# Taking the norm of 256 memory rows inside the last fox pair of a streaming encoder step, and turning the memory columns one projection earlier

## The chip, the cores and the metric

One core of a Trainium2 chip runs the whole program. The metric is the device time of one execution in microseconds (us). Three executions of the kernel before are shown, and one more was recorded by the hardware profiler.

## What is computed

The program is one inference step of a one-layer encoder on 1056 frames (a prompt of 1024 and a sample of 32), with 1024 model columns. What matters here is the part that reads the 256 memory rows:

```python
def _mem_kv(mem, g_mem, w_mem_kv, gk_mem):
    bsz, n, _ = mem.shape
    kv = _rmsnorm(mem, g_mem) @ w_mem_kv
    mk, mv = jnp.split(kv, [MEM_DIM], axis=-1)
    mk = _head_rms(mk.reshape(bsz, n, MEM_HEADS, HEAD_DIM), gk_mem)
    return mk, mv.reshape(bsz, n, MEM_HEADS, HEAD_DIM)
```

`_rmsnorm` divides each memory row by the root of its mean square and multiplies by a gain per column. The layer around it is: a SwiGLU feed-forward block, a norm, one combined projection (a gated convolution of 256 channels, "fox" attention of 8 heads with a forget gate, memory cross-attention of 4 heads), the output projection, a second SwiGLU block and a last norm. Every product is kept near fp32 precision by splitting both factors into a high and a low part and adding three products (hi x hi, hi x lo, lo x hi).

## The kernel before

The kernel is written with one instruction stream per engine, and the order on each engine is the order of the code. TensorE (PE) has the first feed-forward block, two conv groups, four fox pairs of two heads each (`attend(g)`, g = 0 to 3, NG = 4), two memory pairs (`mem_pairs`), the output projection and the second feed-forward block. Engines meet in counting semaphores: `wait_ge(sem, n)` holds an engine's whole stream until the count is there.

**A fox pair** has nine projections, then rows of scores whose maxima VectorE (DVE) takes (`smax(0)` to `smax(17)`), and then 28 blocks n = 0 to 27. For each block PE forms the keyed scores (`keyed(n)`, lines L2782 to L2785), ScalarE (ACT) the exponentials (`exps(n)`, L1480), and PE weighs the values with them (`weigh(n)`, L2814), two blocks behind: the loop runs keyed(n), weigh(n - 2). The outputs gather in PSUM banks. DVE then divides six parts (`mixed(0)` to `mixed(5)`: a reciprocal of the sums at L2254 and a product at L2258), as their last blocks are weighed: after blocks 6, 11, 20, 21, 22 and 27. Each part adds 2 to the count `A["mixed"]`. Block 17 is the sample's first one of the second head, 32 columns wide, and its output goes to bank 0, which part 0 frees; so PE waits for both counts of part 0 there:

```python
                    if q0 == SEQ and first:
                        pe.wait_ge(A["cv_loaded"], 32 * g + 32)
                        if j:
                            pe.wait_ge(A["mixed"], 12 * g + 2)
```

**The memory rows** lie in two tiles by token, `memtok[0]` (a piece of `raw`, shown as w_raw) and `memtok[1]` (mem_by_token), loaded long before. Before the change their norm is the start of the memory pairs. ACT squares and sums both tiles (`memory_rough`, L1538), DVE makes the mean (L2283), ACT the rough root of it (`rough`: a logarithm at L1121 and an exponential at L1123), DVE refines it in three tiny steps (`rstd`, L1736 to L1740) and scales both tiles (L2287). PE turns them by 16 transposes (`turn_memory`, L2651) behind the second of the memory pair's projections, (0,1). They go to banks 3, 4, 5 and 7, of which 4 and 5 hold outputs of the last fox pair until its part 5 is divided (`A["mixed"]` at 12 * NG). DVE multiplies the turned columns by the gain (`memory_gain`, L2180) into the two halves of `memf`: columns 0 to 3 over `mixf` (shown as mix_f), columns 4 to 7 over `vT`. `mixf` has to be stored first (`MIX["stored"]`, an SP transfer at L799). ACT rounds each half (`memory_hi`, L1545), and GpSimd (POOL) takes what is left (L1072, shown as memT_lo).

**What waits for them on PE**: projection (0,2) waits for both halves of the gain (`mp["dve"]` at 6), and the key projection (0,3), which multiplies the memory, for both low halves (`mp["lo"]` at 2). Halfway through each projection PE sums the head squares of the one before (`mem_sums`, L2874).

**POOL** splits weights: a CAST for the high part and a TENSOR_TENSOR for the low one. In the last fox pair it does `split_in` for the first memory pair and then `split_second(0, 1)` and `split_second(1, 2)` (L1060, L1062), four instructions that start when the weights of the second memory pair have landed.

## Time and profile before

| | before |
|---|---|
| three executions, us | 2075.45, 2075.93, 2077.22 |
| median, us | 2075.93 |
| the profiled execution's own time, us | 2075.1 |
| its span in the profile, us | 2073.3 |
| mean granted TensorE clock | 0.994 |
| PE busy | 2019.5 us, 97% of the span |
| DVE busy | 1342.2 us, 65% |
| ACT busy | 967.8 us, 47% |
| POOL busy | 452.5 us, 22% |

All positions below are microseconds from the start of the span. The last fox pair's 28 blocks take 1130 to 1166, the memory pairs 1166 to about 1258. A row of the timeline has its start, its length, the engine, the line, the operation, the tile written and the tiles read, their sizes, how many instructions are merged, and in brackets how long the engine was idle before it and what ended that. PE matmuls overlap each other in these rows. PEclk is the granted share of TensorE's full clock.

### The profile page before, as it was taken

The numbers are of one execution on the slowest core, as the hardware profiler recorded it, in microseconds if no ns is written. First come the engines' busy times: TensorE is split into PE (matmuls) and PEld (weight loads), VectorE is DVE, ScalarE is ACT, GpSimd is POOL, SyncE is SP. The second block draws the span as 40 slices with busy tenths as digits, with TensorE's granted clock in tenths as the row PEclk, the third lists the DMA queues.
The fourth block names the chain that finished last, engine by engine and source line by source line (L and its number), as shares of the span: only waits on it lengthen the run. The fifth ranks groups of instructions, "written<-read, shape, count | busy, mean of one in ns | idle before, by whom it ended". The sixth has DMA issues, their size and how long they took to land.

```text
span 2073.3 us, 35667 instructions
## 1 busy us (share of the span) xinstructions
PE 2019.5 (97%) x14062; PEld 1929.0 (93%) x14062; DVE 1342.2 (65%) x2065; ACT 967.8 (47%) x1643; POOL 452.5 (22%) x225
## 2 busy tenths in 40 slices
PE   5999999999999999999999999999999999999998
PEld 5999999999999999877868779999999999999997
DVE  7999647994415673656666785699965599623323
ACT  6556434654334431445445572266544466533423
POOL 0000000003665744011011342000000000266662
PEclk8999999999999999999999999999999999999999
DMA  7554324555746344621111244064523265474732
GB/s 228 132 148 134 102 64 132 161 155 183 238 162 224 133 156 42 100 78 37 52 48 52 62 159 141 9 203 138 154 85 93 83 189 144 156 259 167 247 133 114
DMA packets 296852, 274.51 MB, mean 132 GB/s; under 512 B 29864, under 2 KB 238888, under 8 KB 296432
## 3 DMA queue, kind: packets, MB, share of 16 engines
q1 hardware_dynamic: 296688, 272.25, 43.7%
q8 instruction: 113, 1.85, 0.4%
q14 instruction: 51, 0.42, 0.1%
HBM read 222.41 MB, written 49.80 MB: 131 GB/s over the span
## 4 chain that ended last, share of the span: by engine, by line
PE 87%; DVE 6%; ACT 3%; issue 1%; another core or an unknown queue 0%; DVEq 0%; ACTq 0%
PE banks L277 26%; PE banks L278 26%; PE banks L279 26%; PE banks L2814 3%; DVE scores_minusF L2245 1%; PE banks L2782 1%; PE banks L2783 1%; PE banks L2736 1%; ACT k_hi_twice L1436 1%; ACT head_r L1121 0%; DVE head_rstd L1738 0%; DVE head_rstd L1736 0%; DVE head_rstd L1740 0%; DVE kT L2210 0%
## 5 line engine op out<-in xcount | busy, mean ns | idle before, releaser
L277 PE MATMUL banks<-hforms_hi,w_hi 128*128 128x264 f32 x2112 | 601.4, 285 | 10.8 <-DVE hforms_lo L1940 6.8
L278 PE MATMUL banks<-hforms_lo,w_hi 128*128 128x264 f32 x2112 | 601.6, 285 | 0.0
L279 PE MATMUL banks<-hforms_hi,w_lo 128*128 128x264 f32 x2112 | 600.3, 284 | 0.0
L1001 POOL TENSOR_TENSOR w_lo<-w_raw,w_hi 128x1024 fp32r<-128x1024 f32 x132 | 321.5, 2439 | 1196.6 <-ACT w_hi L1231 1196.6
L277 PEld LDWEIGHTS banks<-hforms_hi,w_hi 128*128 128x128 f32 x2112 | 398.1, 188 | 14.5 <-issue 7.9
L279 PEld LDWEIGHTS banks<-hforms_hi,w_lo 128*128 128x128 f32 x2112 | 397.4, 188 | 0.0
L278 PEld LDWEIGHTS banks<-hforms_lo,w_hi 128*128 128x128 f32 x2112 | 397.1, 188 | 0.1
L277 PE MATMUL banks<-acts_a,w_hi 128*128 128x352 f32 x960 | 309.9, 323 | 0.0
L279 PE MATMUL banks<-acts_a,w_lo 128*128 128x352 f32 x960 | 309.2, 322 | 0.0
L278 PE MATMUL banks<-acts_a,w_hi 128*128 128x352 f32 x960 | 309.0, 322 | 0.0
L1231 ACT ACTIVATE w_hi<-w_raw 128x1024 fp32r<-128x1024 f32 x132 | 139.5, 1058 | 282.9 <-PE banks L279 259.9
L277 PE MATMUL banks<-h_hi,w_hi 128*128 128x352 f32 x576 | 198.7, 345 | 5.2 <-DVE vT L2180 3.0
L279 PE MATMUL banks<-h_hi,w_lo 128*128 128x352 f32 x576 | 186.6, 324 | 0.0
L278 PE MATMUL banks<-h_lo,w_hi 128*128 128x352 f32 x576 | 186.3, 323 | 0.0
L277 PEld LDWEIGHTS banks<-acts_a,w_hi 128*128 128x128 f32 x960 | 180.3, 188 | 0.2
L278 PEld LDWEIGHTS banks<-acts_a,w_hi 128*128 128x128 f32 x960 | 180.3, 188 | 0.2
L279 PEld LDWEIGHTS banks<-acts_a,w_lo 128*128 128x128 f32 x960 | 180.2, 188 | 0.0
L1163 ACT ACTIVATE w_hi<-w_raw 128x512 fp32r<-128x512 f32 x228 | 142.6, 625 | 54.0 <-PE banks L279 51.8
L1163 ACT ACTIVATE w_hi<-w_sums 128x1024 fp32r<-128x1024 f32 x112 | 118.5, 1058 | 82.0 <-PE banks L279 75.5
L1834 DVE TENSOR_TENSOR w_lo<-w_raw,w_hi 128x512 fp32r<-128x512 f32 x228 | 155.8, 684 | 0.1
L1959 DVE TENSOR_TENSOR acts_a<-acts_f,acts_a 128x704 fp32r<-128x704 f32 x60 | 107.1, 1795 | 59.4 <-ACT acts_a L1219 59.4
L1843 DVE TENSOR_TENSOR w_lo<-w_sums,w_hi 128x1024 fp32r<-128x1024 f32 x112 | 136.4, 1218 | 1.2 <-ACT w_hi L1163 0.9
(343 smaller groups left out, 3560.1 us busy)
## 6 DMA issues: line engine op xcount, KB each, us to landing
w_raw<-in_w_ffn_down SPq DMA_DIRECT2D x132, 512.0 KB, 3.7
w_raw<-in_w_ffn_gate SPq DMA_DIRECT2D x76, 512.0 KB, 5.3
w_raw<-in_w_ffn_up SPq DMA_DIRECT2D x76, 512.0 KB, 5.1
act_rows<-act_f SPq DMA_DIRECT2D x44, 528.0 KB, 3.0
acts_f<-act_rows SPq DMA_DIRECT2D x66, 352.0 KB, 4.1
w_raw<-in_w_in SPq DMA_DIRECT2D x20, 512.0 KB, 5.7
x_spill<-xT SPq DMA_DIRECT2D x4, 2112.0 KB, 10.0
xT<-x_spill SPq DMA_DIRECT2D x6, 1408.0 KB, 9.1
```

The lines of the kernel that those rows point to most:

```text
L277: eng.matmul(out, w_hi, x_hi, start=first, stop=False, skip_group_check=added)
L278: eng.matmul(out, w_hi, x_lo, start=False, stop=False, skip_group_check=added)
L279: return eng.matmul(out, w_lo, x_hi, start=False, stop=last, skip_group_check=added)
L1001: pool.tensor_tensor(wlo[:, wd_slot(e), :], raw[:, wd_slot(e), :], whi[:, wd_slot(e), :].bitcast(F32), ALU.subtract)\
L1163: act.activation(slots(whi, wxh, G[q], n), src, ACT.Copy).then_inc(f[f"{which}_hi"], 1)
L1231: act.activation(whi[:, wd_slot(e), :], raw[:, wd_slot(e), :], ACT.Copy).then_inc(f["wd_hi"], 1)
L1436: act.activation(KS1[half_rows(j), j, s:s + w], kT[half_rows(j), s:s + w], ACT.Copy)\
L1834: dve.tensor_tensor(slots(wlo, wxl, slot, 1), r[:, at:at + 1, :], slots(whi, wxh, slot, 1).bitcast(F32), ALU.subtract).then_inc(f[f"{which ...
L1843: dve.tensor_tensor(slots(wlo, wxl, slot, 2), SS[:, 2 * part:2 * part + 2, :], slots(whi, wxh, slot, 2).bitcast(F32), ALU.subtract)\
L1959: dve.tensor_tensor(acts(p)[:, 1, :, :], astg[:, m % 4, :, :], acts(p)[:, 0, :, :].bitcast(F32), ALU.subtract).then_inc(f["act_lo"], 1)
L2245: dve.tensor_tensor_reduce(junk[0:rows, 0:w], PS[0:rows, b:b + w], nF[0:rows, j, k0:k0 + w], 1.0, -3e38, ALU.add, ALU.max, m).then_inc(A[" ...
L2814: pe.matmul(PS[:, 512 * ob + oc:512 * ob + oc + w], VO[0:kr, vo, j, :], PRT[0:kr, (b0 + n) % 4, 0:w], start=first, stop=last, skip_group_c ...
```

## The change

Four things are moved, and no instruction is added or taken away on any engine.

1. ACT's two squares of the memory rows go from the start of the memory pairs into the last fox pair, ahead of the third piece of maxima (`maxima(2)`), and write to two buffers of `PRT` (probsT). The rough root goes behind `exps(14)`.
2. DVE's mean goes behind `smax(13)`. The three refining steps and the two scalings (`memory_scaled`) go behind the last `smax`, ahead of `mixed(0)`.
3. PE turns the memory columns behind projection (0,0) and no more behind (0,1), in the order 4 to 7, 0 to 3. The wait for the last fox part stays with it.
4. DVE's `memory_gain` comes first in the memory pairs, ahead of `mem_normed(0, 0)`, with columns 4 to 7 (over `vT`) before 0 to 3, so that only the second half waits for the store of `mixf`. ACT and POOL take the halves in that order, the first directly behind the rough root of projection (0,0).

```diff
@@ -1066,8 +1066,8 @@
             pool.wait_ge(W["loaded"], 48 * (MEMV + 1) + 48)
             split_second(0, 1)
             split_second(1, 2)
-            for h in range(2):
-                pool.wait_ge(mp["hi"], h + 1)
+            for h in (1, 0):
+                pool.wait_ge(mp["hi"], 2 - h)
                 ks = slice(4 * h, 4 * h + 4)
                 pool.tensor_tensor(meml[:, ks, :], memf[h], memh[:, ks, :].bitcast(F32), ALU.subtract)\
                     .then_inc(mp["lo"], 1)
@@ -1412,6 +1412,16 @@
                 act.wait_ge(A["mixed"], mem(1, "mixed", 18))
                 act.activation(hh[:, KT - 1, :], mixf[:, :], ACT.Copy).then_inc(MIX["hi_last"], 1)
 
+            def memory_squares(b0):
+
+                act.wait_ge(mp["loaded"], 32)
+                act.wait_ge(A["pv"], b0)
+                for t in range(2):
+                    if t:
+                        act.wait_ge(mp["act"], t)
+                    act.activation(PRT[:, 0:2, :].rearrange("p a n -> p (a n)"), memtok[t], ACT.Square,
+                                   accum_out=tiny[:, t:t + 1]).then_inc(mp["act"], 1)
+
             def attend(g):
                 kind, it = ATTEND[g]
                 proj0, sq0, nrm0, tt0, b0 = (upto(n, g) for n in (NPROJ, NSQ, NRM, NTT, NB))
@@ -1516,11 +1526,16 @@
                 for q in range(1, 5):
                     tokens(q)
                 for x in range(3):
+                    if (g, x) == (NG - 1, 2):
+                        memory_squares(b0)
                     maxima(x)
                 if g == 0:
                     act.wait_ge(fg["copied"], 5)
                 for n in range(NB[kind]):
                     exps(n)
+                    if (g, n) == (NG - 1, 14):
+                        act.wait_ge(mp["dve"], 1)
+                        rough(mp["act"], 2, tiny[:, 2:4], tiny[:, 14:16])
                     if n == max(V_BEHIND):
                         v_copy(8)
                     if n == V_TURNED:
@@ -1530,19 +1545,9 @@
                         if n == TURN2[kind][h]:
                             maxima(3 + h)
 
-            def memory_rough():
-                act.wait_ge(mp["loaded"], 32)
-                for t in range(2):
-                    if t:
-                        act.wait_ge(mp["act"], t)
-                    act.activation(vT[:, 0:D], memtok[t], ACT.Square, accum_out=tiny[:, t:t + 1]).then_inc(mp["act"], 1)
-                act.wait_ge(mp["dve"], 1)
-                rough(mp["act"], 2, tiny[:, 2:4], tiny[:, 14:16])
-
-            def memory_hi():
-                for h in range(2):
-                    act.wait_ge(mp["dve"], 5 + h)
-                    act.activation(memh[:, 4 * h:4 * h + 4, :], memf[h], ACT.Copy).then_inc(mp["hi"], 1)
+            def memory_hi(h):
+                act.wait_ge(mp["dve"], 6 - h)
+                act.activation(memh[:, 4 * h:4 * h + 4, :], memf[h], ACT.Copy).then_inc(mp["hi"], 1)
 
             def mem_squares(p, m):
                 n = MEM_NORMED[p][m]
@@ -1646,11 +1651,11 @@
                 act.activation(lr[r, 0:w], lr[r, 0:w], ACT.Exp, scale=-1.0).then_inc(A["rough_sum"], 1)
 
             def mem_pairs():
-                memory_rough()
                 mem_squares(0, 0)
                 mem_rough(0, 0)
+                memory_hi(1)
                 mem_squares(0, 1)
-                memory_hi()
+                memory_hi(0)
                 mem_rough(0, 1)
                 mem_squares(0, 2)
                 mem_q_hi(0, 0)
@@ -2174,8 +2179,10 @@
 
             def memory_gain():
 
-                for k in range(KT):
-                    dve.wait_ge(mp["turned"], k // 2 + 1)
+                for k in (4, 5, 6, 7, 0, 1, 2, 3):
+                    dve.wait_ge(mp["turned"], (k + 4) % KT // 2 + 1)
+                    if k == 0:
+                        dve.wait_ge(MIX["stored"], 16 * MEMV)
                     b = 512 * TOK_BANK[k // 2] + NMEM * (k % 2)
                     ins = dve.tensor_scalar(memf[k // 4][:, k % 4, :], PS[:, b:b + NMEM], gain[:, 3, k:k + 1], None,
                                             ALU.mult)
@@ -2189,6 +2196,17 @@
                 else:
                     dve.wait_ge(MIX["hi_last"], 1)
                 dve.tensor_tensor(hl[:, b, :], src, hh[:, b, :].bitcast(F32), ALU.subtract).then_inc(MIX["lo"], 1)
+
+            def memory_mean():
+                dve.wait_ge(mp["act"], 2)
+                dve.tensor_scalar(tiny[:, 2:4], tiny[:, 0:2], 1.0 / D, None, ALU.mult).then_inc(mp["dve"], 1)
+
+            def memory_scaled():
+                dve.wait_ge(mp["act"], 4)
+                rstd(mp["dve"], 1, tiny[:, 2:4], tiny[:, 14:16], tiny[:, 12:14])
+                for t in range(2):
+                    dve.tensor_scalar(memtok[t], memtok[t], tiny[:, 12 + t:13 + t], None, ALU.mult)\
+                       .then_inc(mp["scaled"], 1)
 
             def attend(g):
                 kind, it = ATTEND[g]
@@ -2275,17 +2293,12 @@
                 dve.wait_ge(A["minusF_loaded"], 32 * g + 32)
                 for n in range(18):
                     smax(n)
+                    if (g, n) == (NG - 1, 13):
+                        memory_mean()
+                if g == NG - 1:
+                    memory_scaled()
                 for x in range(6):
                     mixed(x)
-
-            def memory_scaled():
-                dve.wait_ge(mp["act"], 2)
-                dve.tensor_scalar(tiny[:, 2:4], tiny[:, 0:2], 1.0 / D, None, ALU.mult).then_inc(mp["dve"], 1)
-                dve.wait_ge(mp["act"], 4)
-                rstd(mp["dve"], 1, tiny[:, 2:4], tiny[:, 14:16], tiny[:, 12:14])
-                for t in range(2):
-                    dve.tensor_scalar(memtok[t], memtok[t], tiny[:, 12 + t:13 + t], None, ALU.mult)\
-                       .then_inc(mp["scaled"], 1)
 
             def mem_normed(p, m):
                 n = MEM_NORMED[p][m]
@@ -2356,10 +2369,8 @@
                    .then_inc(A["mixed"], 1)
 
             def mem_pairs():
-                memory_scaled()
+                memory_gain()
                 mem_normed(0, 0)
-                dve.wait_ge(MIX["stored"], 16 * MEMV)
-                memory_gain()
                 mem_normed(0, 1)
                 mem_q_lo(0, 0)
                 mem_normed(0, 2)
@@ -2645,7 +2656,7 @@
             def turn_memory():
 
                 pe.wait_ge(mp["scaled"], 2)
-                for k in range(KT):
+                for k in (4, 5, 6, 7, 0, 1, 2, 3):
                     for t in range(2):
                         b = 512 * TOK_BANK[k // 2] + NMEM * (k % 2) + t * P
                         mm = pe.transpose(PS[:, b:b + P], memtok[t][:, k * P:(k + 1) * P], ident[:, :])
@@ -3019,7 +3030,7 @@
                     mm = split3(pe, bank(MEM_BANK[p][n], w), w_hi[:, ks], w_lo[:, ks], xh[:, k, s:s + w], xl[:, k, s:s + w],
                                 k == 0, k == KT - 1)
                 mm.then_inc(A["proj"], 1)
-                if (p, n) == (0, 1):
+                if (p, n) == (0, 0):
                     pe.wait_ge(A["mixed"], 12 * NG)
                     turn_memory()
                 if (p, n) == (0, 3):
```

**DVE, between the last maximum and the first division of the last fox pair.** att_, memprep_ and mix_ are the semaphore families `A`, `mp` and `MIX`; the row_max row is the last maximum. Before:

```order
L2245 ISA scores_minusF,row_max<-banks,minusF 128x1024 [waits att_smax,att_scores]
L2245 ISA row_max 128x1
L2254 RECIPROCAL sum_rs<-banks 64x512 [waits att_pv]
L2258 TENSOR_TENSOR mix_f<-banks,sum_rs 64x512 [waits mix_stored,att_mixed]
L2254 RECIPROCAL sum_r<-banks 64x512 [waits att_pv]
```

With the change:

```order
L2263 ISA scores_minusF,row_max<-banks,minusF 128x1024 [waits att_smax,att_scores]
L2263 ISA row_max 128x1
L1741 SCALAR_TENSOR_TENSOR tiny<-tiny 128x2 [waits memprep_act]
L1743 SCALAR_TENSOR_TENSOR tiny<-tiny 128x2 [waits memprep_dve]
L1745 SCALAR_TENSOR_TENSOR tiny<-tiny 128x2 [waits memprep_dve]
L2208 TENSOR_SCALAR w_raw<-w_raw,tiny 128x1024 [waits memprep_dve]
L2208 TENSOR_SCALAR mem_by_token<-mem_by_token,tiny 128x1024
L2272 RECIPROCAL sum_rs<-banks 64x512 [waits att_pv]
L2276 TENSOR_TENSOR mix_f<-banks,sum_rs 64x512 [waits mix_stored,att_mixed]
```

Five instructions now stand ahead of part 0, and the first waits for ACT.

**ACT, blocks 13 to 15 of the last fox pair.** The 128x32 row is exps(14). Before:

```order
L1480 ACTIVATE probsT<-banks,minusF_by_token 128x512 [waits att_pv,att_keyed] x2
L1480 ACTIVATE probsT<-banks,minusF_by_token 128x32 [waits att_pv,att_keyed]
L1480 ACTIVATE probsT<-banks,minusF_by_token 128x128 [waits att_pv,att_keyed]
L1480 ACTIVATE probsT<-banks,minusF_by_token 128x512 [waits att_pv,att_keyed]
L1480 ACTIVATE probsT<-banks,minusF_by_token 128x32 [waits att_pv,att_keyed]
```

With the change:

```order
L1490 ACTIVATE probsT<-banks,minusF_by_token 128x512 [waits att_pv,att_keyed] x2
L1490 ACTIVATE probsT<-banks,minusF_by_token 128x32 [waits att_pv,att_keyed]
L1121 ACTIVATE tiny<-tiny,eps 128x2 [waits memprep_dve]
L1123 ACTIVATE tiny<-tiny 128x2 [waits memprep_act]
L1490 ACTIVATE probsT<-banks,minusF_by_token 128x128 [waits att_pv,att_keyed]
```

The root that DVE waits for is behind the exponentials of block 14.

**PE, blocks 16 and 17 in the last fox pair, with the change.** L2825 is weigh, and L2793 and L2794 are the keyed scores; the same rows stand before the change, at L2814, L2782 and L2783.

```order
L2825 MATMUL banks<-probsT,v_and_ones 128x512 [waits att_expd]
L2793 MATMUL banks<-q_hi_lo,k_hi_twice 128x512 [waits att_expd]
L2794 MATMUL banks<-q_hi_and_max,k_lo_and_one 128x512
L2825 MATMUL banks<-probsT,v_and_ones 128x32 [waits att_mixed,att_cv_loaded,att_expd]
L2793 MATMUL banks<-q_hi_lo,k_hi_twice 32x32 [waits att_expd]
```

The 128x32 weigh is block 17, and its wait for att_mixed is the one for part 0.

## Rows read from the trace of the kernel before

**Rows 1.** The page's part on the chain that ended last: shares by engine

```profile
PE 87%; DVE 6%; ACT 3%; issue 1%; another core or an unknown queue 0%; DVEq 0%; ACTq 0%
```

**Rows 2.** Waits of PE, 1119 to 1240: line waited for, us, times, longest

```profile
PE banks L277 <- DVE vT L2180: 3.0, 1, 3.0
```

**Rows 3.** Timeline of PE: starts of projection (0,1), of the transposes and of (0,2)

```profile
1169.62 0.32 PE L277 MATMUL banks<-h_hi,w_hi 128*128 128x352 f32 x1
...
1174.06 0.27 PE L2651 MATMUL banks<-ident,w_raw 128*128 128x128 f32 x1
...
1178.99 0.40 PE L277 MATMUL banks<-h_hi,w_hi 128*128 128x352 f32 x1 [3.03 <-DVE vT L2180]
```

**Rows 4.** Timeline of DVE: parts 0 and 5, then refining and scaling

```profile
1145.03 3.36 DVE L2254 RECIPROCAL sum_rs<-banks 64x512 f32<-64x512 f32 x1
...
1169.37 0.69 DVE L2258 TENSOR_TENSOR mix_f<-banks,sum_r 64x512 f32<-64x512 f32 x1
...
1170.86 0.16 DVE L1736 SCALAR_TENSOR_TENSOR tiny<-tiny 128x2 f32<-128x2 f32 x1 [0.60 <-ACT tiny L1123]
...
1172.12 0.75 DVE L2287 TENSOR_SCALAR mem_by_token<-mem_by_token,tiny 128x1024 f32<-128x1024 f32 x1
```

**Rows 5.** Timeline of ACT: maxima(2), exps(14), squares, a root

```profile
1129.33 0.59 ACT L1470 ACTIVATE q_hi_and_max<-banks 1x512 fp32r<-1x512 f32 x1 [3.77 <-PE banks L2750]
...
1151.55 0.29 ACT L1480 ACTIVATE probsT<-banks,minusF_by_token 128x32 f32<-128x32 f32 x1
...
1164.47 1.05 ACT L1538 ACTIVATE vT<-w_raw 128x1024 f32<-128x1024 f32 x1
...
1166.61 0.19 ACT L1538 ACTIVATION_READ_ACCUMULATOR vT<-mem_by_token 128x1 f32 x1
...
1172.92 0.50 ACT L1123 ACTIVATE head_r<-head_r 128x352 f32<-128x352 f32 x1
```

**Rows 6.** Timeline of PE: weigh(17), and the last weighs of the pair

```profile
1156.29 0.30 PE L2814 MATMUL banks<-probsT,v_and_ones 128*128 128x32 f32 x2
...
1163.79 2.15 PE L2814 MATMUL banks<-probsT,v_and_ones 128*128 128x512 f32 x6
```

**Rows 7.** Timeline of POOL: second weights, and the memory's second low half

```profile
1152.50 1.04 POOL L1060 CAST w_hi<-w_raw 128x1024 fp32r<-128x1024 f32 x1 [7.74 <-DMA w_raw<-in_w_mem_kv]
1153.61 2.36 POOL L1062 TENSOR_TENSOR second_w_lo<-w_raw,w_hi 128x1024 fp32r<-128x1024 f32 x1
...
1157.04 2.35 POOL L1062 TENSOR_TENSOR second_w_lo<-w_raw,w_lo 128x1024 fp32r<-128x1024 f32 x1
...
1180.79 2.39 POOL L1072 TENSOR_TENSOR memT_lo<-vT,memT_hi 128x1024 fp32r<-128x1024 f32 x1
```

**Rows 8.** Timeline of DVE in the conv groups: the same two instructions twice

```profile
789.57 0.54 DVE L2159 SCALAR_TENSOR_TENSOR qT<-conv_in,conv_weights,qT 128x32 f32<-128x32 f32 x2 [0.48 <-ACT qT L1391]
...
827.01 2.17 DVE L2159 SCALAR_TENSOR_TENSOR qT<-conv_in,conv_weights,qT 128x32 f32<-128x32 f32 x2 [0.48 <-ACT qT L1391]
```

**Rows 9.** Timeline of POOL beside the second of them

```profile
825.64 2.51 POOL L1009 TENSOR_TENSOR w_lo<-w_raw,w_hi 128x1024 fp32r<-128x1024 f32 x1
828.09 1.04 POOL L1026 CAST w_hi<-w_raw 128x1024 fp32r<-128x1024 f32 x1
```

**Rows 10.** Groups of DVE by shape: line, tiles, count, busy us, mean ns

```profile
L1843 DVE TENSOR_TENSOR w_lo<-w_sums,w_hi 128x1024 fp32r<-128x1024 f32 x112 | 136.4, 1218 | 1.2 <-ACT w_hi L1163 0.9
```

**Rows 11.** Timeline of PE: the start again after its longest idle time but the first

```profile
34.30 0.56 PE L277 MATMUL banks<-hforms_hi,w_hi 128*128 128x264 f32 x1 [5.79 <-DVE hforms_lo L1940]
```

**Rows 12.** Windows: us, busy us of PE, PEld, DVE, ACT, POOL, PEclk, DMA share, GB/s

```profile
36.00:38.00 2.00, 2.00 (x6) 1.54 (x6) 1.97 (x5) 0.96 (x2) 0.00 (x0) 0.59 0.14 14
1176.00:1179.00 3.00, 0.01 (x1) 0.04 (x1) 2.85 (x8) 1.18 (x2) 0.55 (x1) 1.00 0.00 0
```

**Rows 13.** DMA issues, 1165 to 1180: KB each, median us to landing

```profile
mix_rows<-mix_f SPq DMA_DIRECT2D x1, 528.0 KB, 2.7
```

## The prediction

> **What bounds the kernel now.** I read the page first: the chain that ended last is 87% PE [rows 1], so only what makes PE wait counts. The waits of PE in the stretch of the change come next: the one wait over 1.5 us is projection (0,2) behind the gain of the memory columns, 3.0 us [rows 2]. The timelines around it show the chain: part 5 of the last fox pair ends at 1170.06, refining and scaling run from 1170.86 to 1172.87 [rows 4], the transposes start at 1174.06, and (0,2) starts at 1178.99 after 3.03 us without work [rows 3]. The change aims at these 3.0 us, which is also the most it can give back: 0.15% of the time. About 0.2% (4.2 us) is what a measurement of this kernel tells from no change. So its gain is small whatever happens, and the question is what the moved work costs where it now stands.
>
> **The change, part by part.**
>
> *Squares on ACT.* They take 2.33 us (1164.47 to 1166.80) and now stand before maxima(2), where ACT idles 3.77 us until 1129.33 [rows 5]. Hidden, 1.4 us to spare; without that cover PE would wait for the maxima by what is missing. The mean, one tiny DVE instruction between two maxima, is hidden in the same way.
>
> *Root on ACT.* It stands behind exps(14), which ends at 1151.84 [rows 5]. Before the change DVE idled 0.60 us for it, from its mean to 1170.86 [rows 4]. So the root is there at about 1152.4. Until then DVE, whose stream now has refining and scaling ahead of part 0, does nothing: before, it began part 0 at 1145.03 [rows 4].
>
> *Refining and scaling on DVE, if nothing holds them.* 2.01 us as before [rows 4], so 1152.4 to 1154.4. Part 0 costs 3.36 + 0.69 and a gap, 4.07 us (part 5's product began 3.38 after its reciprocal), and would be done at 1158.5. PE weighs block 17 at 1156.29 now [rows 6], and that weigh waits for part 0. So PE waits 2.2 us at a place where it didn't wait.
>
> *Refining and scaling beside POOL.* POOL starts splitting the second weights at 1152.50, when they land, and is busy with four instructions until 1159.39 [rows 7]. Before the change POOL was idle when DVE refined and scaled. The conv groups show what such company does: two DVE instructions of 32 columns with both inputs in SBUF take 0.54 us together with no POOL work that reads, and 2.17 us beside POOL [rows 8]. The pair ended at 829.18 [rows 8], just behind POOL's CAST, which ran from 828.09 to 829.13 behind a TENSOR_TENSOR that ended at 828.15 [rows 9]. So I read it as the first instruction held until 828.15 and the second until 829.13. A DVE instruction of this kind then waits for the POOL instruction under way, and POOL's next one gets in before DVE's next: they take turns, however small DVE's instruction is. The three refining steps have both inputs in SBUF (tiny and tiny). The two scalings have one input and no row shows them beside POOL; but 1024 columns take them 0.75 us [rows 4] where a two-input instruction takes 1.22 [rows 10], so they move two columns in the time of one, and I take it that they use both ways into SBUF and are held as well. By turns, with POOL's four instructions against DVE's five: if one step gets through ahead of the CAST at 1152.50, the last scaling comes behind POOL's last instruction, 1159.4 + 0.7 (the first scaling pushes POOL back) + 0.75 = 1160.9. If two get through, it comes behind the second CAST: 1153.7, 1156.1, 1156.9 for the third step, POOL's first low part and the first scaling, 1157.9 for the CAST, 1158.6 for the end. DVE's first step begins within 0.2 us of POOL's CAST, so either can be; I take the middle, 1159.7.
>
> The Trainium skill (SBUF — State Buffer, Who interferes with whom) says that tensor_scalar from SBUF to SBUF can enter a mode with two ports and then contends with GpSimd, the one that issued first holding the pair for its whole instruction. By that rule the scalings are held as I take it; by the rows alone, which show only two-input instructions held, they might not be, and the sum would be rival 2's.
>
> *What PE makes of it.* Part 0 is done at 1159.7 + 4.07 = 1163.8, so weigh(17) waits 7.5 us. The exponentials of blocks 18 and 19 are then ready, which gives back some 0.3. After an idle time of 5.79 us at the start of the kernel PE began again at 34.30 [rows 11], and in 36 to 38 the granted clock was 0.59 on average [rows 12]: with levels of 1.2 and 2.4 GHz that is low for 0.41 / 0.5 x 2 = 1.64 us, until 37.64. Low since 34.30, that is 3.3 us of work at half speed, 1.7 us lost. After the 3.0 us idle time of 1176 to 1179 the clock stayed at 1.00 [rows 12]. 7.5 us are beyond the first of these, so I add the clock's fall: 2.0 us, between 0 (it stays) and about 3.6 (twice as long low).
>
> *Turning the columns.* Shifts so far: 7.5 - 0.3 + 2.0 = 9.2 us on PE. The pair's last weighs end at 1165.94 + 9.2 = 1175.1 [rows 6], and projection (0,0) where (0,1) now begins, 1169.62 + 9.2 = 1178.8 [rows 3]. DVE: part 5 can't begin before the last weigh, 1175.2, and is done at 1179.3, and banks 4 and 5 are free only then: PE waits 0.5 before the transposes, which take 1.8 us (they are 16, and 1175.96, where the idle time of rows 3 begins, less 1174.06 is 1.9), to 1181.1.
>
> *Gain behind (0,1).* DVE gains columns 4 to 7 from about 1179.9, the store lands 2.7 us after part 5 [rows 13], at 1182.0, and the second half is done by 1183.7. Projection (0,1) takes 4.44 us (1169.62 to 1174.06) [rows 3], to 1185.5. So the 3.03 us wait is gone, with 1.8 us to spare.
>
> *What is late next: the low halves on POOL.* They start behind ACT's root of projection (0,0), which ends 3.8 us after (0,1) begins (1169.62 and 1173.42 [rows 3, 5]): 1184.9, ACT rounds to 1186.0, and POOL needs 2 x 2.39 [rows 7], to 1190.8. PE is through (0,2), as long as (0,1), at 1190.0: 0.8 us of wait at (0,3), where the waits of PE show none before. The split of the second query weights behind them on POOL moves with it; projection (1,2) needs it some 10 us later. SP's transfers keep their order, and the store waits only for part 5.
>
> *Sum.* -3.0 (wait at (0,2)) + 7.5 (weigh(17)) - 0.3 + 2.0 (clock) + 0.5 (banks) + 0.8 (low halves) = +7.5. Behind 1191 all engines are late by about the same, and I see nothing that would give it back but tenths (DVE and ACT reach (0,3) less late than PE), so +7.3. The profiled execution took 2075.1 (span 2073.3 and 1.8 around it); the median of the three is 0.8 above it. 2075.9 + 7.3 = **2083.2 us**, 0.35% slower. Its own range: -1.1 and +1.1 for the count of steps that get through, -2.0 and +1.6 for the clock: 2080 to 2086.
>
> **The rivals.**
>
> 1. *Nothing is held, not slower.* POOL doesn't hold instructions of two columns, or the weights land so late that DVE is through first. For it: the first refining step comes within 0.2 us of the CAST, the landing is a transfer's and can vary. Against it: rows 8. DVE would have to be ahead of POOL's start by 2.0 us, so it decides at a landing after 1154.4, 1.9 us later than in the trace. Then +2.2 (weigh(17)) - 0.3 + 0.7 (banks: part 5 ends at 1172.2, projection (0,0) at 1169.62 + 1.9) + 0.6 (low halves) - 3.0 = +0.2: 2076.1.
> 2. *Only the three steps are held, not the scalings.* The third step ends behind POOL's first low part at 1156.1, the scalings at 1157.6, part 0 at 1161.7: weigh(17) waits 5.4 us, just under the idle time of rows 11, so the clock may fall or not. 5.4 - 0.3 + (0 to 2.0) + 1.3 - 3.0 = +3.4 to +5.4: 2079.3 to 2081.3.
> 3. *The gain comes through.* Part 0 is not needed by block 17 as I read it, or PE's 2.2 us are covered. Against it: the wait is in the code, and weighs follow each other without idle time there. -3.0: 2072.9, which is within 0.2%.
>
> **How the numbers follow.** Forecast 0.60, rival 1 0.18, rival 2 0.14, rival 3 0.03, and 0.05 for something not seen, of which most would be slower. Slower by over 0.2% (above 2080.1): 0.57 of the forecast, 0.08 of rival 2, 0.03 of the rest, 0.68. Within 0.2%: 0.03 of the forecast, rival 1 and 3, 0.06 of rival 2, 0.30. Faster: 0.02. The range has to take in rival 1, since without it over 0.2 is left out: 2075.4 to 2086.0.
>
> **What the profile after would show.** Right: DVE's refining steps each far over 0.16 us, ending with POOL's instructions; the last scaling ends between 1158 and 1161; PE idle for 6 to 9 us before the 128x32 weigh, put down to the product of part 0; PEclk under 1.00 in the windows behind it; no wait of (0,2), a short one of the transposes, and a short one of (0,3) for memT_lo. Wrong: refining and scaling 2 us long in all beside POOL (rival 1), scalings of 0.75 us beside a POOL instruction (rival 2), no wait of the 128x32 weigh (rival 3), or a full clock behind the wait, which takes 2 us off.

## The result and the profile after

| | before | after |
|---|---|---|
| executions beside each other, us | 2075.45 to 2077.55 (5) | 2082.52 to 2087.63 (5) |
| median, us | 2076.51 | 2085.09 |
| ratio, 95% interval | | 1.0041 [1.0031, 1.0052] |
| the profiled execution's own time, us | 2075.1 | 2084.51 |
| its span, us | 2073.3 | 2082.7 |
| mean granted TensorE clock | 0.994 | 0.991 |

The change makes the kernel 0.41% slower, by 8.6 us; a second comparison, told below, gave 1.0036 [1.0023, 1.0050]. The prediction was 2083.2 us, in a range of 2075.4 to 2086.0.

The waits of PE from 1119 to 1240 come first, as in [rows 2]: the line that waited, what it waited for, us in total, times, the longest.

```profile
PE banks L2825 <- DVE mix_f L2276: 5.8, 1, 5.8
...
PE banks L277 <- POOL memT_lo L1072: 0.9, 1, 0.9
...
PE banks L2662 <- DVE mix_f L2276: 0.3, 1, 0.3
```

The 3.0 us of (0,2) [rows 2] are gone. In their place stand 5.8 us of weigh(17) for part 0, 0.9 us of (0,3) for the low halves, and 0.3 us of the transposes for part 5. That is 7.0 us for 3.0, or +4.0; the span grew by 9.4. The timeline of PE shows where the rest is: weigh(17), projection (0,0), the transposes and (0,3).

```profile
1162.49 0.61 PE L2825 MATMUL banks<-probsT,v_and_ones 128*128 128x32 f32 x2 [5.81 <-DVE mix_f L2276]
...
1176.40 0.62 PE L277 MATMUL banks<-h_hi,w_hi 128*128 128x352 f32 x1
...
1181.03 0.33 PE L2662 MATMUL banks<-ident,w_raw 128*128 128x128 f32 x1 [0.33 <-DVE mix_f L2276]
...
1192.82 0.36 PE L277 MATMUL banks<-memT_hi,w_hi 128*128 128x256 f32 x1 [0.94 <-POOL memT_lo L1072]
```

From weigh(17) to (0,0) PE takes 13.91 us (1162.49 to 1176.40). Before, the same work took 9.20, from 1156.29 [rows 6] to this line of the timeline of PE of the kernel before:

```profile
1165.49 0.62 PE L277 MATMUL banks<-h_hi,w_hi 128*128 128x352 f32 x1
```

4.7 us for the same instructions, with no wait named. The windows of the kernel after say what it is (us, busy us of PE, PEld, DVE, ACT, POOL, PEclk, DMA share, GB/s):

```profile
1157.00:1159.00 2.00, 0.00 (x0) 0.00 (x0) 1.97 (x2) 0.40 (x1) 1.92 (x2) 1.00 0.00 0
1159.00:1160.00 1.00, 0.00 (x0) 0.00 (x0) 1.00 (x1) 0.00 (x0) 1.00 (x1) 0.64 0.00 0
1160.00:1172.00 12.00, 9.51 (x27) 6.21 (x28) 7.53 (x9) 2.19 (x5) 0.43 (x1) 0.50 0.00 0
1172.00:1173.00 1.00, 1.00 (x4) 0.48 (x3) 1.00 (x1) 0.11 (x1) 0.00 (x0) 0.54 0.00 0
1173.00:1176.00 3.00, 3.00 (x14) 1.82 (x14) 2.95 (x2) 1.63 (x3) 0.00 (x0) 1.00 0.00 0
```

PE was idle from 1156.68. The granted clock fell to 1.2 GHz at about 1159.3 (0.64 in a window of 1 us is 0.72 us at half) and was back at 2.4 GHz at about 1172.9, 10.4 us after PE had work again. So the path closes. The wait begins 0.39 us later than weigh(17) stood before, it lasts 5.81, and the slow clock costs 4.71. From (0,0) to (0,3) PE takes 16.42 us where it took 18.02 (1165.49 to 1183.51, the start of (0,3) before), which is -1.60. The sum is +9.31, and (0,3) begins 9.31 us later. From there to the end of the span both take 889.8 us or 0.1 more: nothing comes back and nothing is added.

Why part 0 is late is on DVE:

```profile
1152.51 0.16 DVE L1741 SCALAR_TENSOR_TENSOR tiny<-tiny 128x2 f32<-128x2 f32 x1 [7.31 <-ACT tiny L1123]
1152.71 0.16 DVE L1743 SCALAR_TENSOR_TENSOR tiny<-tiny 128x2 f32<-128x2 f32 x1
1152.90 0.91 DVE L1745 SCALAR_TENSOR_TENSOR tiny<-tiny 128x2 f32<-128x2 f32 x1
1153.85 2.94 DVE L2208 TENSOR_SCALAR w_raw<-w_raw,tiny 128x1024 f32<-128x1024 f32 x1
1156.71 1.52 DVE L2208 TENSOR_SCALAR mem_by_token<-mem_by_token,tiny 128x1024 f32<-128x1024 f32 x1
1158.26 3.36 DVE L2272 RECIPROCAL sum_rs<-banks 64x512 f32<-64x512 f32 x1
1161.66 0.68 DVE L2276 TENSOR_TENSOR mix_f<-banks,sum_rs 64x512 f32<-64x512 f32 x1
```

and on POOL beside it:

```profile
1152.76 1.04 POOL L1060 CAST w_hi<-w_raw 128x1024 fp32r<-128x1024 f32 x1 [7.77 <-DMA w_raw<-in_w_mem_kv]
1153.88 2.36 POOL L1062 TENSOR_TENSOR second_w_lo<-w_raw,w_hi 128x1024 fp32r<-128x1024 f32 x1
1156.19 1.50 POOL L1060 CAST w_lo<-w_raw 128x1024 fp32r<-128x1024 f32 x1
1157.77 2.67 POOL L1062 TENSOR_TENSOR second_w_lo<-w_raw,w_lo 128x1024 fp32r<-128x1024 f32 x1
```

Read them by turns. Two refining steps aren't held; the second begins 0.05 us ahead of the CAST. The third has 0.16 us of work and takes 0.91, to the end of the CAST (1153.80). The first scaling stands behind the TENSOR_TENSOR until 1156.24 and ends 0.55 us behind it: 2.94 us for 0.75 [rows 4]. POOL's second CAST, pushed by it, takes 1.50 us for 1.04 [rows 7]; the second scaling waits for it and takes 1.52; and POOL's last instruction is pushed in its turn. Refining and scaling take 5.7 us instead of 2.0.

The three new stretches on ACT and DVE ahead of that cost nothing, though the mean was held too: 128 x 2 elements beside a TENSOR_TENSOR of POOL that ran from 1135.75 to 1138.12.

```profile
1137.14 1.01 DVE L2202 TENSOR_SCALAR tiny<-tiny 128x2 f32<-128x2 f32 x1
```

The same instruction in the kernel before, where POOL was idle:

```profile
1170.10 0.17 DVE L2283 TENSOR_SCALAR tiny<-tiny 128x2 f32<-128x2 f32 x1
```

The maxima of the next rows followed at once. The wait of weigh(17) begins 0.39 us later than weigh(17) stood before, and at 1127 PE was 0.24 us later already.

### The profile page after: what moved, and what is told of

The parts are those of the page before. It is cut to its first block, busy times and chain, and to the rows that moved or that the text cites. A ratio compares the mean times of both kernels' runs of the same rounds, so it can differ in the third digit from the quotient of the medians.

```text
span 2082.7 us, 35668 instructions
## 1 busy us (share of the span) xinstructions
PE 2024.9 (97%) x14062; PEld 1932.2 (93%) x14062; DVE 1349.8 (65%) x2065; ACT 969.1 (47%) x1643; POOL 453.9 (22%) x225
## 4 chain that ended last, share of the span: by engine, by line
PE 86%; DVE 6%; ACT 4%; issue 1%; another core or an unknown queue 0%; POOL 0%; DVEq 0%; ACTq 0%
PE banks L277 26%; PE banks L278 26%; PE banks L279 26%; PE banks L2825 3%; DVE scores_minusF L2263 1%; PE banks L2793 1%; PE banks L2794 1%; PE banks L2747 1%; ACT k_hi_twice L1446 1%; ACT head_r L1121 0%; DVE kT L2228 0%; DVE head_rstd L1743 0%; DVE head_rstd L1745 0%; DVE head_rstd L1741 0%
```

## The experiments

Times are medians with their count; ratios are against executions of the kernel before on the same chip, with the 95% interval. The table at the end sets the paths side by side.

### POOL out of the way

```diff
+            pool.wait_ge(mp["scaled"], 2)
             split_second(0, 1)
             split_second(1, 2)
```

> The changed kernel, but POOL starts on the second weights only when both scalings are done; DVE then refines and scales with POOL idle. My theory (the wait at weigh(17) is long because DVE and POOL take turns): refining and scaling take about 2.0 us and end near 1154.6 (1158.2 in the changed kernel), part 0 near 1158.7, weigh(17) waits about 2.2 us instead of 5.8, the clock stays at 1.00 behind it, and the time is the time before +0.2 to +1.0: 2076.7 to 2077.5, 7.5 to 8.5 below the changed kernel. Rival (five instructions and a root ahead of part 0 take this long by themselves, POOL is only in step with them): as the changed kernel, 2085. Rival (the splits of the second weights, now 2.1 us later, are missed): a new wait of PE on second_w_lo or w_hi in the second memory pair.

Measured: 2079.65 us (11), ratio 1.0012 [1.0004, 1.0021]; the executions lie at 2075.02 and 2075.36, and then from 2078.53 to 2082.20. The profiled one took 2082.20. DVE in it:

```profile
1153.75 0.16 DVE L1742 SCALAR_TENSOR_TENSOR tiny<-tiny 128x2 f32<-128x2 f32 x1 [7.30 <-ACT tiny L1124]
1153.94 0.16 DVE L1744 SCALAR_TENSOR_TENSOR tiny<-tiny 128x2 f32<-128x2 f32 x1
1154.14 0.16 DVE L1746 SCALAR_TENSOR_TENSOR tiny<-tiny 128x2 f32<-128x2 f32 x1
1154.34 0.75 DVE L2209 TENSOR_SCALAR w_raw<-w_raw,tiny 128x1024 f32<-128x1024 f32 x1
1155.00 0.75 DVE L2209 TENSOR_SCALAR mem_by_token<-mem_by_token,tiny 128x1024 f32<-128x1024 f32 x1
```

The same five instructions take 2.0 us, and weigh(17) waits 2.1 us. Both numbers were expected, and the rival that POOL is only in step with them falls. The time was not: it is 2.2 us over the upper end of the range. The windows of this trace show what was missed.

```profile
1160.00:1161.00 1.00, 0.99 (x8) 0.83 (x8) 1.00 (x1) 0.28 (x1) 0.92 (x2) 1.00 0.00 0
1161.00:1162.00 1.00, 1.00 (x7) 0.69 (x5) 1.00 (x1) 0.28 (x1) 1.00 (x1) 0.94 0.00 0
1162.00:1172.00 10.00, 10.00 (x27) 6.03 (x26) 6.98 (x8) 2.79 (x5) 0.77 (x1) 0.50 0.00 0
1172.00:1173.00 1.00, 1.00 (x5) 0.51 (x4) 0.09 (x1) 0.50 (x1) 0.00 (x0) 0.94 0.00 0
```

After a wait of only 2.1 us the clock fell too, and it fell when PE had been busy for 1.9 us again (weigh(17) at 1160.01, the fall at about 1161.9). PE took 13.98 us from weigh(17) to (0,0). That the kernel before kept its clock behind 3.0 us [rows 12] is thus no bound.

### PE kept busy over the wait

Products whose result is overwritten are added; nothing is left out.

```diff
                     pe.wait_ge(A["expd"], b0 + n + 1)
+                    if (g, n) == (NG - 1, 17):
+                        for _ in range(24):
+                            pe.matmul(bank(6, 512), KS1[:, 0, 0:P], Q1[:, 0, 0:512], start=True, stop=True)
```

> The changed kernel, and PE does 24 products of 512 columns more between the exponentials of block 17 and weigh(17), about 5.1 us at full clock in the 5.8 us in which it waits; their result goes to a bank that the next block's scores overwrite, so nothing that is computed changes. My theory (4 of the 9.3 us are the clock that fell because PE was idle): the 128x32 weigh still starts near 1162.5 and still waits for part 0, but the clock stays at 1.00 behind it, the last weigh ends near 1172.2 instead of 1176.2, and the time is about 4 us below the changed kernel, 2081 (2080.3 to 2082). Rival (the longer time of blocks 17 to 27 is not the clock but other engines' work, or the clock falls all the same): 2085. Rival (the products fill more than the wait): above 2082, with no wait left at weigh(17).

> The changed kernel with PE kept busy over the wait, unchanged, for a second trace: its profiled run took 2082.5 and the ten others 2078.2 to 2080.2. By the path from weigh(17) to (0,3) it should be the kernel before +4.4. My theory: the profiled run was long by falls of the clock elsewhere (at 48 and at 1256), and this trace shows 2078 to 2080 with POOL and DVE by turns as before. Rival (how many of DVE's steps get through ahead of POOL varies from run to run): part 0 is done more than 0.5 us earlier against the start of the wait.

Measured: 2078.76 us (11), ratio 1.0012 [1.0003, 1.0021]; the second trace's execution took 2080.23. PE and its windows in the second trace:

```profile
1162.98 0.38 PE L2828 MATMUL banks<-probsT,v_and_ones 128*128 128x32 f32 x2 [0.24 <-DVE mix_f L2276]
```

```profile
1157.00:1163.00 6.00, 5.76 (x26) 4.36 (x24) 5.90 (x5) 0.69 (x1) 3.90 (x2) 1.00 0.00 0
1163.00:1176.00 13.00, 13.00 (x67) 9.60 (x68) 12.29 (x9) 3.93 (x8) 0.00 (x0) 1.00 0.05 11
```

The 24 products take 5.8 us and leave 0.2 of the wait. Part 0 is as late as in the changed kernel, weigh(17) starts where it would have, but the clock stays at 1.00, and in both traces PE takes 9.28 us from weigh(17) to (0,0) where the changed kernel takes 13.91. So the 4.7 us are the clock, all but at most 0.1. The time came out 6 us under the changed kernel, not 4: below the range, and below what the path gives against the kernel before (+4.4). The same surplus turns up in other kernels below and is taken up under "What the kernel before pays behind its own wait". DVE's and POOL's turns were the same in both traces (two steps through, and part 0's reciprocal 5.74 and 5.78 us behind the start of the first), so the rival of the second run falls. Its 2080.23 us are 0.2 over what was forecast for it.

### Late without POOL

```diff
+            pool.wait_ge(mp["scaled"], 2)
             split_second(0, 1)
...
                     dve.wait_ge(A["pv"], b0 + n + 1)
+                    if (g, x) == (NG - 1, 0):
+                        dve.reciprocal(lr[r, 0:w], PS[l, b:b + w])
                     dve.reciprocal(over[r, 0:w], PS[l, b:b + w]).then_inc(A["mixed"], 1)
```

> As the first kernel (POOL waits for the scalings), and DVE takes the reciprocal of part 0 twice, the first time into a buffer that part 1 overwrites: 3.4 us of DVE more, so part 0 is done near 1162.1, as late as in the changed kernel, but with no POOL instruction beside refining and scaling. My theory (lateness of part 0 alone does it, whatever its cause): weigh(17) waits about 5.6 us, the clock falls as in the changed kernel, and the time is 2085 (2084 to 2086). Rival (the lateness costs only itself, and the fall of the clock came from something else in the changed kernel): 2081. Rival (POOL's company costs elsewhere too, such as slower reciprocals or mixes): below 2084, by what those rows show.

Measured: 2085.13 us (5), ratio 1.0039 [1.0027, 1.0052], as forecast. Refining and scaling take 2.0 us again, and weigh(17) waits 5.3. The clock is low for 13.6 us, as long as in the changed kernel, but it falls later against the wait: 12.9 of these us lie behind the start of weigh(17) and not 10.4, and PE takes 15.14 us to (0,0):

```profile
1162.00:1175.00 13.00, 12.37 (x33) 7.46 (x33) 8.56 (x8) 2.88 (x6) 0.17 (x1) 0.50 0.00 0
```

With part 0 late for another cause, the loss is that of the changed kernel. So what POOL does to the time, it does by making DVE late.

### Each half of the change alone

Norm at its old place, earlier turn kept (squares, mean, root and `memory_scaled` back at the start of the memory pairs):

```diff
             def mem_pairs():
+                memory_mean()
+                memory_scaled()
                 memory_gain()
```

> Only the second half of the change: the squares, the mean, the root, refining and scaling stand where they stood before the change (at the start of the memory pairs), while the columns are turned behind projection (0,0), the gain comes first on DVE and columns 4 to 7 go first. My theory (the whole loss sits in the moved norm, and the earlier turn by itself moves the wait instead of removing it): no wait at weigh(17), PE waits 3.3 us for the scaled rows before the transposes, (0,2) doesn't wait, (0,3) waits about 0.9 us for the low halves, and the time is the time before +1.0: 2077.5 (2076.5 to 2078.5). Rival (the earlier turn costs by itself, for instance in DVE, ACT and POOL crowding behind it): above 2079.

Measured: 2078.73 us (11), ratio 1.0011 [1.0003, 1.0020]. Waits of PE from 1150 to 1200:

```profile
PE banks L2658 <- DVE mem_by_token L2206: 3.2, 1, 3.2
PE banks L277 <- POOL memT_lo L1072: 0.9, 1, 0.9
```

The earlier turn by itself moves the wait of 3.0 us from (0,2) to the transposes and adds that for the low halves. The time is 0.2 us over the range. In this trace the clock holds behind the wait; whether it holds in the others isn't seen. By the path to (0,3) the earlier turn alone costs 1.3 us.

Norm moved, turn at its old place:

```diff
-                if (p, n) == (0, 0):
+                if (p, n) == (0, 1):
                     pe.wait_ge(A["mixed"], 12 * NG)
                     turn_memory()
```

> Only the first half of the change: the norm is taken in the last fox pair, but the columns are turned behind (0,1) again (with a wait for the last transpose ahead of POOL's low halves, which is met by then). My theory (the norm's place makes the loss, the turn's place takes 3.0 us off and puts 0.3 + 0.9 back): weigh(17) waits 5.8 us and the clock falls as in the changed kernel, no wait at the transposes, (0,2) waits 3.0 us, (0,3) doesn't wait, so the changed kernel +1.8: 2086.3 (2085.3 to 2087.5). Rival (the earlier turn gives nothing net): 2084.2 to 2085.1, as the changed kernel.

Measured: 2086.98 us (5), ratio 1.0048 [1.0034, 1.0061], inside the range. Waits of PE from 1150 to 1200:

```profile
PE banks L2826 <- DVE mix_f L2277: 5.7, 1, 5.7
PE banks L277 <- DVE mix_f L2188: 2.1, 1, 2.1
```

(0,2) waits 2.1 us and not 3.0: DVE gains the columns first here, where in the kernel before the norm of (0,0) stands ahead of the gain (1173.45 to 1175.71). The large loss, the wait at weigh(17) and the clock, sits in the norm's new place. What the turn's new place is worth depends on that: with the norm moved it takes 0.8 us off the path to (0,3) and 1.2 behind it, and with the norm at its old place it costs 1.3.

### The norm behind part 1

DVE has idle time a little later. In the trace of the kernel before it is free from the end of part 1 (1155.50) until part 2:

```profile
1159.40 0.36 DVE L2254 RECIPROCAL sum_rs<-banks 64x32 f32<-64x32 f32 x1 [3.90 <-PE banks L2814]
```

So refining and scaling go there, with POOL behind them:

```diff
-                if g == NG - 1:
-                    memory_scaled()
                 for x in range(6):
                     mixed(x)
+                    if (g, x) == (NG - 1, 1):
+                        memory_scaled()
...
+            pool.wait_ge(mp["scaled"], 2)
             split_second(0, 1)
```

> The changed kernel with two moves: DVE refines and scales behind part 1 of the last fox pair instead of ahead of part 0, where it had nothing to do until part 2 (about 1155.5 to 1159.4), and POOL's second weights wait for the scalings. My theory (the whole price of the change sits in part 0 being late): the 128x32 weigh of block 17 doesn't wait, the clock stays at 1.00 up to the transposes, (0,2) doesn't wait, what is left is 0.3 us at the transposes (banks 4 and 5) and 0.9 us at (0,3), so -3.0 + 0.3 + 0.9 = -1.8: 2074.8 (2074 to 2076), at least 1.5 us below the kernel before. Rival (the delay of POOL's second weights or of part 2 to 5 is missed on PE): a new wait there, 2077 or more.

Measured: 2073.20 us (11), ratio 0.9985 [0.9976, 0.9993]. The time is 0.8 us below the range, and the path is as forecast: weigh(17) doesn't wait, the transposes wait 0.3 us and (0,3) 0.9.

The same with POOL where the changed kernel has it:

> The changed kernel with refining and scaling behind part 1 (about 1155.5), and POOL's second weights where they were, from about 1152.5 to 1159.4. Part 2 is not wanted before 1159.4. My theory (DVE and POOL still take turns, but idle time of DVE covers it now): a refining step and both scalings far over 0.16 and 0.75 us, ending between 1159.4 and 1161, parts 2 and 3 up to 1.5 us late and not missed, the 128x32 weigh without a wait, and the same time as the kernel with POOL behind the scalings: 2073.2 (2072.5 to 2074.2). Rival (being held costs there too, through parts 2 to 5): 2074.5 or more, with a longer wait at the transposes.

Measured: 2074.39 us (11), ratio 0.9987 [0.9978, 0.9996]. DVE in it:

```profile
1154.74 0.64 DVE L1741 SCALAR_TENSOR_TENSOR tiny<-tiny 128x2 f32<-128x2 f32 x1
1155.41 0.95 DVE L1743 SCALAR_TENSOR_TENSOR tiny<-tiny 128x2 f32<-128x2 f32 x1
1156.39 0.16 DVE L1745 SCALAR_TENSOR_TENSOR tiny<-tiny 128x2 f32<-128x2 f32 x1
1156.59 2.74 DVE L2208 TENSOR_SCALAR w_raw<-w_raw,tiny 128x1024 f32<-128x1024 f32 x1
```

DVE is held by POOL here just as in the changed kernel, for some 3 us, and weigh(17) doesn't wait. The second scaling wasn't held (0.74 us), though the forecast had both held. The path from weigh(17) to (0,3) is the same to 0.05 us with and without POOL beside it (25.68 and 25.63). The median is 0.2 us over the range, and the two intervals overlap: the runs don't tell the two kernels apart. Being held costs nothing that these runs can show where no one waits for DVE.

Then the first high half goes ahead of ACT's root, so that POOL starts earlier:

```diff
-                mem_rough(0, 0)
                 memory_hi(1)
+                mem_rough(0, 0)
                 mem_squares(0, 1)
...
                 pool.wait_ge(mp["hi"], 2 - h)
+                pool.wait_ge(mp["turned"], KT // 2)
```

> The same as the kernel with the scalings behind part 1, and ACT rounds the first half of the memory ahead of the rough root of projection (0,0) instead of behind it, so that POOL can start on the low halves about 1.5 to 3 us earlier; a wait for the last transpose is added ahead of POOL's low halves, which is met by then. My theory: the 0.9 us at (0,3) goes too, the root of (0,0) moves back by at most 1 us and is not missed, so -3.0 + 0.3 = -2.7: 2073.9 (2073.2 to 2075.5). Rival (the rounding, which must wait for DVE's gain, holds ACT's root and with it DVE's norm and the head squares): (0,3) or a later projection waits for ACT or DVE instead, 2075 or more.

Measured: 2072.23 us (11), from 2071.19 to 2073.19, ratio 0.9978 [0.9969, 0.9987]. The time is 1.0 us below the range. This version beats both kernels: 4.4 us under the kernel before (2.7 to 6.4 by the interval), some 12 to 13 under the changed one. Of PE's waits from 1150 to 1200 one is left:

```profile
PE banks L2664 <- DVE mix_f L2278: 0.3, 1, 0.3
```

But its path is only 2.7 us shorter than that of the kernel before, and the one above only 1.6 (3.4 measured). Both gained 1.7 to 1.8 us more than their paths give.

### What the kernel before pays behind its own wait

```diff
                 elif p == 0:
+                    if n == 2:
+                        for _ in range(12):
+                            pe.matmul(bank(2, 512), w_hi[:, 0:P], hh[:, 0, 0:512], start=True, stop=True)
                     pe.wait_ge(mp["dve"], 6)
```

> The kernel before, and PE does 12 products of 512 columns more ahead of projection (0,2), about 2.9 us in its 3.0 us of idle time; their result is overwritten by the projection, so nothing that is computed changes. The two kernels without idle time there came out 3.4 and 4.4 us below the kernel before, where their paths give 1.8 and 2.7. My theory (in most executions of the kernel before, though not in the profiled one, the clock also falls behind the 3.0 us wait and costs 1 to 2 us in the median): 2075.0 (2074.3 to 2075.7), 1 to 2 us below the kernel before on the same chip, with the same path. Rival (the 1.7 us come from elsewhere in the two kernels): as the kernel before, 2076.6, or 0.1 to 0.3 more.

> The kernel before, unchanged, for a second trace. Theory of the clock: with an even chance or better, PEclk under 1.00 in windows between 1176 and 1200 in this trace, and then 2076 to 2078; else 2074 to 2076. Rival: 1.00 there and still 2076.5 or more.

Measured: 2075.03 us (11) against 2076.84 (21) of the kernel before in this comparison, ratio 0.9992 [0.9984, 1.0001]; the second trace of the kernel before has 2076.58. Its windows:

```profile
1176.00:1179.00 3.00, 0.23 (x1) 0.26 (x2) 2.62 (x7) 1.40 (x2) 0.78 (x1) 1.00 0.00 0
1179.00:1180.00 1.00, 1.00 (x5) 1.00 (x5) 0.00 (x0) 0.72 (x1) 1.00 (x1) 0.51 0.00 0
1180.00:1182.00 2.00, 2.00 (x9) 2.00 (x8) 0.00 (x0) 0.00 (x0) 2.00 (x2) 0.50 0.00 0
1182.00:1183.00 1.00, 1.00 (x5) 0.79 (x4) 0.00 (x0) 0.00 (x0) 0.91 (x1) 0.78 0.00 0
```

The same kernel, the same 3.0 us wait at the same place, and this time the clock falls at about 1179.0 and is back at 1182.4; PE takes 19.58 us from (0,0) to (0,3) instead of 18.02. So the kernel before pays for its 3.0 us twice in some executions, and a kernel without the wait gains both. How often it does two traces don't tell. In the median this comparison gives 1.8 us, with an interval that just reaches 1 (3.3 us less to 0.2 more). That is an estimate and no price of the fall: the one fall seen here cost 1.6 us, which is the most that it could give even if it came each time.

### A second trace of the changed kernel

> The changed kernel, unchanged, for a second trace of it. In the first runs it took 2082.5 to 2087.6, and in the run in which PE waited only 2.1 us at weigh(17) the clock fell too. My theory (the clock's fall behind the wait of 5.8 us comes in each execution or nearly, with a start and a length that vary): again about 10 to 14 us at 0.50 from 1157 to 1163 on, and 2083 to 2087. Rival (it comes only sometimes, and the median is a mixture): a clock of 1.00 behind the wait and 2080 to 2081.

Measured: 2084.24 us (4), ratio 1.0036 [1.0023, 1.0050], as forecast. The wait is 5.7 us, the clock is low from about 1158.5 to 1172.1, and PE takes 13.87 us from weigh(17) to (0,0). One step gets through ahead of POOL's CAST here, and not two:

```profile
1151.86 0.16 DVE L1741 SCALAR_TENSOR_TENSOR tiny<-tiny 128x2 f32<-128x2 f32 x1 [7.30 <-ACT tiny L1123]
1152.06 1.03 DVE L1743 SCALAR_TENSOR_TENSOR tiny<-tiny 128x2 f32<-128x2 f32 x1
1153.13 0.16 DVE L1745 SCALAR_TENSOR_TENSOR tiny<-tiny 128x2 f32<-128x2 f32 x1
1153.32 2.75 DVE L2208 TENSOR_SCALAR w_raw<-w_raw,tiny 128x1024 f32<-128x1024 f32 x1
```

and it makes no difference. POOL's CAST ends at 1153.08 and its TENSOR_TENSOR begins at 1153.16; the third step, begun at 1153.13, is still ahead of it and takes its 0.16 us, and the first scaling is held as before. With the turn at its old place it was the same (one step through, the second 0.97 us).

### The paths side by side

Worked out from each trace's timeline of PE: the wait at weigh(17), the start of weigh(17) to that of (0,0), (0,0) to (0,3), and (0,3) to the end of the span, in us. The last column is the median less that of the kernel before in the same comparison.

| kernel | wait | to (0,0) | to (0,3) | to the end | measured |
|---|---|---|---|---|---|
| before | 0 | 9.20 | 18.02 | 889.8 | |
| before, second trace | 0 | 9.20 | 19.58 | 889.9 | |
| before, PE kept busy | 0 | 9.20 | 17.97 | 889.7 | -1.8 |
| changed | 5.81 | 13.91 | 16.42 | 889.9 | +8.6 |
| changed, second trace | 5.73 | 13.87 | 16.43 | 889.7 | +7.7 |
| changed, PE kept busy | (5.95 filled) | 9.28 | 16.43 | 891.4 | +2.2 |
| changed, PE kept busy, second trace | (filled) | 9.28 | 16.43 | 889.7 | |
| POOL behind | 2.09 | 13.98 | 16.42 | 889.8 | +3.0 |
| late without POOL | 5.30 | 15.14 | 16.41 | 889.8 | +8.5 |
| norm at the old place | 0 | 9.20 | 19.29 | 891.4 | +2.1 |
| turn at the old place | 5.68 | 14.91 | 17.23 | 891.0 | +10.1 |
| part 1 first, POOL as it was | 0 | 9.20 | 16.48 | 890.0 | -2.5 |
| part 1 first, POOL behind | 0 | 9.20 | 16.43 | 889.9 | -3.4 |
| and the high half first | 0 | 9.20 | 15.34 | 889.7 | -4.4 |

If the kernel before pays some 1.8 us in the median, the paths come near the times of the kernels that don't idle at weigh(17) or (0,2): +4.4 - 1.8 = +2.6 (measured +2.2), -1.6 - 1.8 = -3.4 (-3.4), -2.7 - 1.8 = -4.5 (-4.4). The kernel with part 1 first and POOL as it was doesn't fit as well: -1.5 - 1.8 = -3.3 for a measured -2.5. POOL behind gives +0.5 - 1.8 = -1.3 without a fall, 2075.3, where its two quickest executions lie, and 4.8 more with one, 2080.1, in the middle of the other nine.

The losses from weigh(17) to (0,0) differ by how much of the low clock falls on work. Behind the start of weigh(17) the clock was low for 10.2, 10.4, 10.4, 12.5 and 12.9 us (POOL behind, changed twice, turn at the old place, late without POOL), and PE took 4.8, 4.7, 4.7, 5.7 and 5.9 us more: 0.45 to 0.47 us for each.

The two ends of 891.4 (PE kept busy, first trace, and norm at the old place) hold a fall of the clock of 3.4 us at 1257.4 and 1253.5, some 0.6 us behind a wait of 1.4 us (L3084 and L3077, for `mix_f`). All fourteen traces have that wait, 1.4 us each time, and in twelve the clock stayed at 1.00. The fall cost 1.6 us each time. So 0.9 us of the kernel with the norm at its old place, which its path leaves open even if it pays 1.8 behind its own 3.2 us (+1.3 measured against +2.1), may be falls at this second place; that isn't shown. The end of 891.0 (turn at the old place) has no fall: by 1211 it has already lost 1.0 us more than the changed kernel, in small steps at head sums and transposes of the memory pairs, of which the profile names one wait of 0.25 us (L2894 for DVE's `kT`).

## Why the prediction was right, and where its sum was not

Its forecast came in: slower by over 0.2%, by the mechanism it named first. Step by step:

- *Squares, mean, root.* The squares and the mean are hidden, the root is there at 1152.5 (1152.4 forecast). Right. That the mean was "hidden in the same way" was right too, but not thought of as held by POOL.
- *Unheld, 2.2 us at weigh(17).* Shown by the kernel with POOL behind: 2.0 us of refining and scaling, 2.1 us of wait.
- *By turns with POOL.* Shown: held in each of the five traces with both engines at it ahead of part 0, and not in the two without. The price was 1.5 us too high, because the prediction took the middle between one step through (1160.9) and two (1158.6). Two got through, and the end was 1158.2, 5.72 us behind the start of the first step. In the second trace one got through, and the end was 5.65 us behind it and not 2.3 later, as the two branches had it. The step that failed is "POOL's next one gets in before DVE's next": in the traces with one step through (the second of the changed kernel, and the turn at its old place) the third step, of 0.16 us, came between the CAST and POOL's next. And a scaling ended 0.55 us behind the instruction that held it, where the sum took 0.7 to 0.8. Wait at weigh(17): 5.8 for 7.5.
- *The Trainium skill (SBUF — State Buffer, Who interferes with whom)* was weighed for the scalings, which have one input. By its rule they would be held; the rows before didn't show it. The trace agrees with it: 2.94 and 1.52 us for 0.75. Rival 2 falls.
- *-0.3 behind the wait.* Not seen: with the clock at 1.00 PE took 9.28 us from weigh(17) to (0,0), 0.1 more than before and not 0.3 less.
- *The clock, +2.0, between 0 and 3.6.* Mis-sized, and its largest error: +4.6 were measured (4.7 less the 0.1 above), beyond its upper end, though the fall itself came as forecast. The failed step is "low since 34.30, that is 3.3 us of work at half speed". The kernel before has these windows there:

```profile
30.00:32.00 2.00, 0.00 (x0) 0.00 (x0) 1.93 (x5) 2.00 (x2) 0.00 (x0) 0.70 0.90 344
32.00:34.00 2.00, 0.00 (x0) 0.00 (x0) 2.00 (x2) 2.00 (x2) 0.00 (x0) 0.50 1.05 401
```

  The clock was low from about 30.8, while PE was still idle, to 37.6: 6.8 us, of which only the last 3.3 fell on work. The prediction took that share for the size of a fall. In the changed kernel 13.6 us were low and 10.4 of them fell on work, for some 4 (7 at most) in the sum. In the five traces with a wait at weigh(17) and a fall behind it PE took 4.7, 4.7, 4.8, 5.7 and 5.9 us more to (0,0), and the fall in the kernel before cost 1.6. Why a low stretch was 3.4 us long in one place and 13.6 in another stays open.
- *"7.5 us are beyond the first of these."* The reading behind it, that idle times up to 3.0 us leave the clock alone, is wrong: it fell behind 2.1 us and, in the second trace, behind the same 3.0 us from which it was read; and twice behind 1.4.
- *Turn, gain, low halves.* 0.3 at the transposes for 0.5, 0.94 at (0,3) for 0.8, no wait at (0,2); together -1.60 for -1.7. Right.
- *"The most it can give back", 3.0 us.* The best version gave 4.4, with an interval of 2.7 to 6.4, so that it gives more than the wait is likely and not shown.
- *The sum.* +7.5 forecast; the trace has +8.9 and a start 0.4 later. 5.8 for 7.5 and 4.7 for 1.7 (2.0 less 0.3) have opposite signs and in part offset each other, so that the total is closer than its terms is luck. And the path of one execution was set on the median: what the kernel before loses more in the median than in that execution (some 1.8 us by the estimate above) isn't in the sum.

The rival "nothing is held" was given 2076.1 us and within 0.2%. Its condition was tried, and the median is 2079.65: with the wait that it too had, 2.2 us, the clock fell in the traced execution, and nine of the eleven times lie around the 2080.1 that a fall gives. It was priced without a clock.

## What to carry to other kernels

Before small work is moved into a gap on an engine, look at what the engine does directly after the gap and who waits for that: the same five instructions cost some 10 us of PE's path ahead of part 0 (5.8 + 4.7) and nothing behind part 1, POOL beside them or not. Price an idle time of PE as itself and a possible fall of the clock behind it, which cost 1.6 us behind waits of 1.4 and 3.0, 4.8 behind one of 2.1, and 4.7 to 5.9 behind 5.3 to 5.8. What counts is the part of the low clock that falls on work: some 0.46 us for each us of it. Where one trace shows no fall, take a second before you rest on it, and compare medians with medians.
